# Where the latents' out-gate and value columns are projected: ahead of the scans, or in the beats beside them

## What is computed

```python
h = rmsnorm(x, g1) * (1.0 + sc1) + sh1
aq, ai, aff, afb, ag, bq, bk, bv, ga, gb = split_columns(h @ w_in)
# mixer A: two-directional gated scan of q, k = 1 - f, values ai;
#          then per-head rmsnorm, times silu(ag)
o_a, s_f, s_b = hgrn2_mixer(aq, ai, aff, afb, ag, lb_f, lb_b, a_norm, s0_f, s0_b)
# mixer B: banded attention of axial_rope(q), axial_rope(k), v
o_b = latent_window_attention(axial_rope(q), axial_rope(k), v, ctx_k, ctx_v, sink)
y = (sigmoid(ga) * (o_a @ w_oa) + sigmoid(gb) * (o_b @ w_ob)) @ w_out
x = x + gt1 * y
x = x + gt2 * peer(h2)      # 128 experts a token: u = p_u[idx]; v = p_v[idx]
```

## Time and profile before

| | |
|---|---|
| median of three executions | 2533.73 us |
| profiled execution | 2531.67 us |
| its span, first to last instruction | 2529.9 us |
| busy of the span: PE, DVE, ACT, POOL | 2007.2, 1749.0, 977.8, 940.1 us |
| mean granted TensorE clock | 0.923 of full |
| stage win, about | 320 to 526 us |
| stage merged | 526 to 911 us |
| stage mix | 911 to 1081 us |

### The profile page before, as it was taken

How to read it: one execution, slowest core, us unless ns; L and a number is a source line. 1 busy time by engine, 2 the same in 40 slices (tenths; PEclk the granted TensorE clock), 3 DMA queues, 4 the chain that set the end, 5 groups by cost and what they waited for, 6 DMA issues and landing times. The chain is left out here.

```text
span 2529.9 us, 27355 instructions
## 1 busy us (share of the span) xinstructions
PE 2007.2 (79%) x6925; PEld 1115.7 (44%) x6925; DVE 1749.0 (69%) x3969; ACT 977.8 (39%) x2481; POOL 940.1 (37%) x774
## 2 busy tenths in 40 slices
PE   6978899946566679988698876877878787787876
PEld 2677846835555544476454222322223222232222
DVE  2732278888776768667787777777777777777764
ACT  1402145244444344412333434444444444344443
POOL 0020012222221222202233554656645665456654
PEclk9998999968787789989899999999989999899999
DMA  8844678853332369959798999999999999999997
GB/s 323 289 150 157 224 294 332 306 187 131 116 101 100 117 234 345 340 213 402 270 374 318 421 422 390 422 422 422 421 403 422 422 422 421 403 414 422 422 422 323
DMA packets 113299, 805.53 MB, mean 318 GB/s; under 512 B 12596, under 2 KB 14006, under 8 KB 17046
## 3 DMA queue, kind: packets, MB, share of 16 engines
q0 software_dynamic: 93760, 680.96, 67.3%
q1 hardware_dynamic: 17704, 118.17, 12.7%
q10 hardware_dynamic: 1712, 4.98, 0.5%
HBM read 800.79 MB, written 3.28 MB: 318 GB/s over the span
## 5 line engine op out<-in xcount | busy, mean ns | idle before, releaser
L1213 POOL DMA_INDIRECT RG<-in_uv,idxs x264 | 357.9, 1356 | 561.6 <-DVE pl L1440 326.9
L957 ACT ACTIVATE agel<-apre 128x1 f32<-128x1 f32 x640 | 129.2, 202 | 944.8 <-DVE apre L1412 940.9
L600 PE MATMUL pl<-RG,BP 128*128 128x512 f32 x576 | 296.6, 641 | 106.8 <-ACT BP L973 103.5
L600 PE MATMUL pl<-RING,BP 128*128 128x512 f32 x576 | 282.0, 621 | 60.7 <-ACT BP L973 57.7
L1412 DVE CUSTOM_DVE_ANT_0 R<-RG,AB 128x1024 f32<-128x1024 f32 x201 | 246.6, 1230 | 103.5 <-DMA RG<-in_uv,idxs 84.3
L1213 POOL DMA_INDIRECT RING<-in_uv,idxs x168 | 248.1, 1477 | 159.3 <-issue 71.0
L1412 DVE CUSTOM_DVE_ANT_0 R<-RING,AB 128x1024 f32<-128x1024 f32 x168 | 206.0, 1226 | 95.1 <-DMA RING<-in_uv,idxs 77.4
L625 PE MATMUL pa<-HL,RING 128*128 128x512 f32 (+2 forms) x800 | 243.3, 461 | 1.1 <-DMA RING<-in_pq_slabs 1.0
L600 PEld LDWEIGHTS pl<-RG,BP 128*128 128x128 f32 x576 | 100.4, 193 | 295.8 <-ACT BP L973 219.2
L973 ACT ACTIVATE BP<-CT,wexp 128x128 f32<-128x128 f32 x480 | 192.7, 401 | 47.8 <-PE pl L600 9.9
L600 PEld LDWEIGHTS pl<-RING,BP 128*128 128x128 f32 x576 | 104.4, 194 | 232.5 <-ACT BP L973 135.0
(11 more groups left out here) (288 smaller groups left out, 3285.6 us busy)
## 6 DMA issues: line engine op xcount, KB each, us to landing
RING<-in_in_slabs SPq DMA_DIRECT2D x42, 1024.0 KB
RING<-in_pq_slabs SPq DMA_DIRECT2D x24, 1152.0 KB
RING<-in_ada_slabs SPq DMA_DIRECT2D x16, 1024.0 KB
RING<-in_out_slabs SPq DMA_DIRECT2D x12, 1024.0 KB
RG<-in_col_slabs POOLq DMA_DIRECT2D x8, 1024.0 KB, 7.0
RING<-in_o_slabs SPq DMA_DIRECT2D x8, 1024.0 KB
RG<-in_uv,idxs POOLq DMA_INDIRECT x297, 6.1
RING<-in_uv,idxs POOLq DMA_INDIRECT x168
```

The costliest lines, as they stand in the source:

```text
L600: last = nc.tensor.matmul(acc[:, c * 512:(c + 1) * 512], DG[:, k % 2, :], bufs[k % len(bufs)][:, D + c * 512:D + (c + 1) * 512], start=Fal ...
L957: A(agel[:, par, k:k + 1], apre[:, par, k:k + 1], ACT.Gelu).then_inc(gel_done, 1)
L1213: nc.gpsimd.indirect_dma_start(out=bufs[b], out_offset=None, in_=uv, in_offset=bass.IndirectOffsetOnAxis(ap=idxs[:, par, k:k + 1], axis=0) ...
```

## The change

The latents' projections are reordered: BQ 0, BQ 1 and BKV come first, then the twelve turned groups, then I 0. The slabs AG 0, AG 1 and I 1 (`DEFERRED`) are projected in merged: twelve groups (3 slabs x 4 tiles), one in each of the first twelve beats, 0 to 11 (nine of unit 1 and three of unit 2), between scores and turned probabilities. They turn through the four banks instead of the six. Their three slabs use one RING buffer, the one that held the first merge-gate slab; each is loaded when its predecessor's last group is done. Slots: 40 in win, 42 in merged, 46 in mix, instead of 46, 40, 42. On DVE the rotary steps are spread over the turned groups of q and the first forget gate, and both forget passes come after them. The SiLU of the out-gates comes in the last beat of unit 1, `out_gate` moves to unit 2, and PE waits for all values at the tail of unit 3 instead of ahead of `turn_qk`. POOL goes on with slots up to I 0 before it waits for the forget gates.

```diff
+WIN_FIRST, WIN_LAST = WIN[:3], WIN[3:4]
+DEFERRED = [(W_AG, 0), (W_AG, 1), (W_I, 1)]
+DEFER = [(w, a, t) for w, a in DEFERRED for t in range(1, NT)]
-STAGES = (("win", 46, {"winT": 6.0, "win": 3.0}),
-          ("merged", 40, {"diag": 1.0, "lvl": 1.0, ...
-          ("mix", 42, {"oT": 1.0, "gate_a": 6.9, ...
+STAGES = (("win", 40, {"winT": 6.0, "win": 3.0}),
+          ("merged", 42, {"win": 0.0, "diag": 1.0, "lvl": 1.0, ...
+          ("mix", 46, {"oT": 1.0, "gate_a": 6.9, ...
...
+            SLABS += ([("winD", w, a) for w, a in DEFERRED] if (_b, _q) == (1, 0) else [])
...
-        SLABS += [("winTL", w, m) for w in WIN_T for m in range(2)] + [("winL", w, a) for w, a in WIN]
+        SLABS += ([("winL", w, a) for w, a in WIN_FIRST] + [("winTL", w, m) for w in WIN_T for m in range(2)]
+                  + [("winL", w, a) for w, a in WIN_LAST])
+SLAB_SLOT, _pos = {}, 0
+for _key in SLABS:
+    SLAB_SLOT[_key] = _pos % NSLAB
+    _pos += _key[0] != "winD"
...
+def beside_scores(piece, n):
+
+    for w, a, t in DEFER[n - HB:n - HB + 1] if n >= HB else ():
+        piece(w, a, t)
...
     if name[0] == "win":
-        return name[3] > 0
+        return name[3] > 0 and name[1:3] not in DEFERRED
...
-        while names[at + 1][0] in ("pT", "oB"):
+        while names[at + 1][0] in ("pT", "oB") or (names[at + 1][0] == "win" and names[at + 1][1:3] in DEFERRED):
...
             for n, key in enumerate(SLABS):
-                if n >= NSLAB:
-                    wait_full(sp, last_use(SLABS[n - NSLAB]))
+                if before[key]:
+                    wait_full(sp, last_use(before[key]))
...
                 if i == 0:
+                    if v == 3:
+                        pe.wait_ge(win_ready[W_I], 2 * NT)
...
                 if n < hi:
                     scores(n)
+                if lo:
+                    beside_scores(lambda w, a, t: win("winD", [(w, a)], [t]), n)
...
-            win("winL", range(1, NT))
-            pe.wait_ge(win_ready[W_I], 2 * NT)
+            win("winL", WIN_LAST, range(1, NT))
+            pe.wait_ge(win_ready[W_I], 2 + LAT // P)
...
                 if i == 2:
+                    if 0 < v < NT - 1:
+                        beside.before(("lvl", v + 1, i + 1, 1))
...
+                if lo_:
+                    beside_scores(lambda w, a, t: win(w, a, [t]), n)
+                    if n == beat_of(1, BEATS - 1):
+                        gates_on()
...
-            beside.before(("win", W_AG, 0, 1))
+            beside.before(("win", W_I, 0, 1))
...
-                    if u == 1 and l < NT - 1:
+                    if u == 2 and l < NT - 1:
                         out_gate(l + 1)
...
-            for d in range(2):
-                beside.before(("winT", WIN_T[1 + d], 3))
-                forget(d, 1)
             dve.wait_ge(rot_in, 16)
-            later = [("win", wc, a, t) for wc, a in ((W_I, 0), (W_I, 1), (W_AG, 0)) for t in range(1, NT)]
+            later = [("winT", wc, m) for wc in WIN_T[:2] for m in range(4)]
...
                 dve.sem_inc(rope_ready, 1)
+            for d in range(2):
+                beside.before(("winT", WIN_T[1 + d], 3))
+                forget(d, 1)
```

More of the change, by code:

```diff
@@ L151, in attention_beat @@
             names.append(("sc", n))
+        if lo:
+            beside_scores(lambda w, a, t: names.append(("win", w, a, t)), n)
         if lo <= n - 2 < hi:
@@ L192, in plan_groups @@
     marks = [len(names)]
+    names.extend(("win", w, a, t) for w, a in WIN_FIRST for t in range(1, NT))
     names.extend(("winT", w, m) for w in WIN_T for m in range(4))
-    names.extend(("win", w, a, t) for w, a in WIN for t in range(1, NT))
+    names.extend(("win", w, a, t) for w, a in WIN_LAST for t in range(1, NT))
     marks.append(len(names))
@@ L513, in half_update @@
             yield mul(tots[:, set_of(u), d, :] if l == LEVELS - 1 else HT[d][l % 2][:, 0:n], T2[:, :, 0], T2[:, :, 1])
[L515 to L518, removed]
+        slab_turn, before, counts, last_in = {}, {}, [0] * NSLAB, [None] * NSLAB
+        for key in SLABS:
+            i = SLAB_SLOT[key]
+            counts[i] += 16
+            slab_turn[key] = (i, counts[i])
+            before[key], last_in[i] = last_in[i], key
         block = ctx.enter_context(nc.Block())
@@ L530, in last_use @@
                     return ("winP" if kind == "winT" else "winT", key[1], 2 * key[2] + 1)
-                if kind in ("win", "winL"):
+                if kind in ("win", "winL", "winD"):
                     return ("win", key[1], key[2], 0 if kind == "win" else NT - 1)
@@ L551, in _ @@
                     src = ada_slabs[ADA_SEGS[key[1] // 4] * 4 + key[1] % 4]
-                elif kind in ("win", "winL", "winT", "winTL"):
+                elif kind in ("win", "winL", "winD", "winT", "winTL"):
                     src = in_slabs[key[1] // SC_W + key[2]]
@@ L677, in _, with win @@
             win_turned("winT", "winP", hTp, P)
-            def win(kind, tiles):
-                for wc, a in WIN:
+            def win(kind, which, tiles):
+                for wc, a in which:
                     w = chunks(slab(kind, wc, a))
@@ L686, in win @@
                         finish(("win", wc, a, t), last)
-            win("win", [0])
+            win("win", WIN, [0])
             pe.wait_ge(win_ready[W_I], 2)
@@ L907, in _ @@
             pe.wait_ge(hT_ready, NT)
+            win("winL", WIN_FIRST, range(1, NT))
             win_turned("winTL", "winT", hTl, LAT)
-            win("winL", range(1, NT))
-            pe.wait_ge(win_ready[W_I], 2 * NT)
+            win("winL", WIN_LAST, range(1, NT))
+            pe.wait_ge(win_ready[W_I], 2 + LAT // P)
             turn_qk([1, 2, 3, 4])
@@ L1078, in turn_qk, with gates_on @@
                     step(A(KT(t), ps[:, 512:640], ACT.Copy), *freed(("qkT", t)), qkT_ready)
-                if tiles[0]:
-                    for t in tiles:
-                        step(A(OA(t), OA(t), ACT.Silu), ag_ready)
+            def gates_on():
+                for t in range(1, NT):
+                    step(A(OA(t), OA(t), ACT.Silu), ag_ready)
             def attention_beat(n, lo_, hi_):
@@ L1164, in _ @@
             act.wait_ge(mk_ready, 1)
+            for wc, a in WIN_FIRST:
+                win(wc, a, range(1, NT))
             for wc, dst, fn, ready in WT:
```

14 lines of the change are left out of this document (8 added, 6 removed).

## The result

| | before | after |
|---|---|---|
| median of six executions | 2535.29 us | 2542.12 us |
| lowest, highest | 2530.89, 2540.07 | 2539.49, 2545.21 |
| span of the profiled execution | 2529.9 us | 2539.6 us |
| win / merged / mix of the profiled execution | 205.9 / 385.0 / 171.1 us | 178.5 / 415.7 / 182.4 us |

After over before is 1.0029, 95% interval 1.0015 to 1.0042. The kernel became slower by 6.8 us; 2532 had been forecast.

The account below looks back on a forecast made before the run. It took DVE to end win, short DVE-PE handovers to bound merged and PE to bound mix. Terms -20 - 2 + 7 + 11 + 3 = -1 us gave 2532 us; band 2526 to 2541, 8-in-10 range 2515 to 2552.

Parts of the forecast that it names:

- Step 1: Latents' in-projections (win): six slots leave, and DVE ends the stretch earlier; -20 us (-17 to -24).
- Step 2: Start of the scan: queries are turned early with PE ahead, saving DVE's wait for PE; -2 us (0 to -4).
- Step 3: Scan with attention (merged): two more slots lengthen beats on DVE, the busiest engine; +7 us (+4 to +8).
- Step 4: First twelve beats of merged: one projection group in each, partly hidden; +11 us (-5 to +30).
- the 7 us taken off for a faster clock: First twelve beats: half of the low-clock stretches rise, making PE's part of each round 0.6 us shorter; -7 us.
- The bank order: Beats with a slot: turned probabilities take that beat's score banks and wait for DVE's row maximum; about +9 us.
- The slab at beat 8: Beat 8 of merged: PE waits 1 to 3.5 us for the third slab; +5 us with its group.
- DVE waits for PE where there was none: Expected sign in the profile after: new DVE waits for PE in merged's first twelve beats; no size given.
- Step 5: Merge stage (mix): four more slots come under PE's 170 us; +3 us (0 to +10).
- A: Merged: the projections vanish in PE's idle gaps; -14 us in all, 2519 us; chance 0.34.
- B: First beats of merged: PE sets the pace, groups delay level blocks; +18 us in all, 2551 us; chance 0.23.
- C: Win: DVE stays at 526 us because something else ends last; +15 to +20 us, 2550 us; chance 0.06.

Follow-up runs that it names:

- Slots only: The kernel before with the changed slot counts (40, 42, 46) and no projection moved; 2528.74 us, ratio 0.998 to the kernel before.
- the projections alone: The kernel after with the slot counts of before (46, 40, 42); 2556.81 us, ratio 1.0087 to the kernel before.
- the two like profiles: The kernel after with slots 82 to 127 gathering half of each row (2533.27 us), or summing half of the columns (2536.82 us).
- the thin projections: The kernel after with one matmul of eight in each moved group: 2537.73 us; also with eleven groups in bank 4: 2522.17 us.
- a third kernel: The kernel after with ten moved groups in bank 4, slots 34/52/42 and no projection in beat 8; 2517.83 us, ratio 0.9938 to before.

## Why the prediction was wrong

The sum of the stages was to be -1 us and is +14.6 (-27.4, +30.7, +11.3), less 4.9 for an early start and a shorter rest. Two terms failed, the fourth and the fifth, both in the same direction; the first three held to within 2 us, and win gave some 7 us that no term had.

**Step 1 (six slots leave win, -20): right.** Slots only gives -20.4, so 3.4 us a slot. The whole -27.4 has another 7.0 us in it from the projections, fewer of them and in another order; the projections alone show 6.4 (199.5 against 205.9 with 46 slots in both). I had said that the reordering costs nothing and not asked whether it gives something. DVE's waits for gathered rows fell (RG from 7.8 us to 4.0), which goes that way but is only part of it. PE waits 27.5 us for ScalarE at the end of win, where some 40 were named and 16.7 stood before:

```profile
491.78 1.10 PE L649 MATMUL pa<-CT,AB 128*128 128x128 f32 x4 [27.54 <-ACTq L475]
```

**Step 2 (turned queries early, -2): not seen.** From the scan's first DVE operation to its first matmul it is 5.4 us before and 5.4 after:

```profile
495.19 0.43 DVE L1621 TENSOR_SCALAR HG<-AB 128x512 f32<-128x512 f32 x1 [0.25 <-DVE gws L1424]
```

```profile
500.54 3.41 PE L646 MATMUL pa<-AB,HG 128*128 128x128 f32 x16
```

The turned blocks did begin ahead of that operation, at 491.78, but the last of them stands at 499.45, 3.12 us behind ScalarE, and the scan's first matmul comes after it. PE was through with its projections at 464 us (458.84 and 5.41) and had nothing of it: these blocks are tied to ScalarE's order, and ScalarE's to the slots.

**Step 3 (two slots more in merged, +7): right**, +6.2, though merged read from one profile is no surer than 3 us.

**Step 4 (twelve groups in twelve beats, +11): mis-sized; it is +24.5** (18.2 and 22.2 with the two like profiles). This is the step that failed. The mechanism it named, the turned probabilities in the banks of the same beat's scores, stands in the bank table and in beat 2, and its range to +30 holds the price. The step in it that failed for certain is the 7 us taken off for a faster clock. The clock did rise: 0.85 after in the first twelve beats, where before had 0.77 and slots only 0.70. But the thin projections show what this is worth. With the groups in bank 4 their matmuls raise the granted clock from 0.73 to 0.88, and the twelve beats are still 6.8 us longer than without them (155.9 against 149.1): the higher clock is already in that. The 18 us before the credit lie at the lower end of what was measured. The bank order, which I took at 9 us, is 15.0 by the one pair of profiles, 12.1 against the mean of the like ones, and 8.4 to 12.4 by the timed runs; it was about right or too small. The rest of the sum (4.3 for PE's rounds and 5 for the slab) agrees with the 8.8 of PE's time. What the Trainium skill says of the clock ("TensorE: Matmul & The Clock Gate", section "What's actually happening"), that activity releases the throttle, agrees with these rows; that a released throttle shortens the stretch doesn't follow from it. The slab at beat 8, 5 us in the sum, is the wait of 2.53 us below, with a wait of DVE for the take of 8.9 us in the view above, where slots only has 3.6: 5.3 us more, as summed. At another slot count the two waits were 5.7 and 12.1.

```profile
599.84 6.67 PE L646 MATMUL pa<-RING,HL 128*128 128x256 f32 x16 [2.53 <-DMA RING<-in_in_slabs]
```

The growth was in the first twelve beats alone, as foretold, though 13.8 us of it came with the slots. The prediction's sign "DVE waits for PE where there was none" was misread: the kernel before has 8.2 us of such waits there.

**Step 5 (four slots more in mix, +3): mis-sized; it is +11.3, and +14.6 in slots only.** The prediction called this kind of growth wrong in kind, from 10 up. The numbers stood there: 180 us if all of DVE's idle time recurred, and 163 without its 27 us of waits; that second number is a slip, since 180 less 27.3 is 153. I assumed that the waits shrink once DVE is late, and gave no reason. They recurred: 18.2 us for RG, 10.1 for EB, another buffer, and 6.7 for the weights, 35.0 in all; before, it was 17.0, 7.4 (a row that I had not listed) and 10.3, 34.7 in all. In the stage as a whole DVE does 12.8 us more work (126.7 to 139.5) and idles as long as before (44.4 and 42.9), which is the 11.3 us. Rows that come late don't come earlier because the engine that asks for them is later; each gather is issued only when a sum has freed its buffer. Mix had room on DVE by busy time (125.5 of 170), but DVE was already waiting there for its rows, at a DMA share of 0.86, 0.88 after.

**The rivals.** A (faster) fell with merged at 415.7. B had the sign (slower), its +29 for term 4 lay closer to 24.5 than my own 11, and merged at 415.7 is by the prediction's own mark (415 or more) B. Its mechanism, PE's time alone, is a part: 8.8 us beside 15.0 for the banks in the profiles, 5.8 to 9.9 beside 8.4 to 12.4 by the timed runs. Its total of 2551 counted 4 for mix and 20 for win. C fell with win at -27.4. That the total lies within the range is a balance of errors: 5.4 us more gain in win than my -22, 12.7 more loss in merged than +18 and 8.3 more in mix than +3.

## What to carry to other kernels

Before a group is put into a fixed order of accumulation banks, list which bank each later group then takes and who must have read it: one more group shifts every pair behind it, and a bank outside the rotation, if one is free for that long, avoids it. Before a transfer-fed task is moved under a long stage, read the waits for its data there and not only the busy time of its engine: waits for a buffer loop recur with each further task. And split a change in two, because here one half was worth 6 us alone and the other alone cost 22, and a third kernel with the useful part of each was 15 us faster.

## What the runs showed of the hardware

- Added matmuls raised the granted clock of the stretch that they stand in: with 42 slots in merged it is 0.70 in the first twelve beats without the projections, 0.73 with one matmul in eight of them, and 0.85 to 0.88 with all. It was not enough to pay for them: in bank 4 the stretch at 0.88 took 6.8 us more than that at 0.73.
- Gathers of 1 MB (128 rows of 8 KB) came too late for DVE in mix at a DMA share of 0.85 to 0.88 and 323 to 329 GB/s, though 343 were reached in the same stage with less work between them. They landed 7.6 us after their issue (median), with half of each row's bytes 4.9; then the share was 0.62, and the stage was at PE's length.
- A slab of 1 MB, asked for when the last group on its buffer was done, was usable 8.45 us after that group's end (7.0 us from issue to landing was the nearest row before), and the group that had waited for it took 6.58 us (granted clock 0.56 in that stretch) instead of 3.72 (1.00).
